# Forget gates by token-stationary matmuls, and two steps of the second attention layer in another place

## The chip, the core and the metric

The kernel runs on one core of a Trainium2 chip. The metric is the time on the device of one execution, in microseconds; of several runs the median counts. Five engines with an instruction queue each work side by side: TensorE (PE, with its weight loads shown apart as PEld), VectorE (DVE), ScalarE (ACT), GpSimd (POOL) and SyncE (SP, whose queue here issues nearly all DMAs). They wait for each other by semaphores.

## What is computed

Two blocks of a transformer for 256 tokens of width 1024, all in fp32: first a block with latent attention, a Fourier mixer and 32 experts, then two layers more, one that mixes two sparse attentions and has an MLP, and one with forgetting attention ("FoX") and an MLP. The change lies in the FoX layer. In the terms of the code, with h the normalised tokens (256 x 1024):

```
q, k, v, z = split(h @ odd_w_in)      # widths 1024, 1024, 1024, 16 (one z per head)
f   = log_sigmoid(z + b_forget)       # 256 x 16, as min(z, 0) - log(1 + exp(-|z|))
cum = cumsum(f, over tokens)
s[h, i, j] = q_i . k_j / 8 + cum[i, h] - cum[j, h]    for j <= i
out = softmax(s) @ v;   x = x + out @ odd_w_out
```

## The kernel before

The program is written engine by engine: each block (`block.tensor`, `block.vector` and so on) is the queue of one engine in the order in which it is written, and a step starts when those ahead of it in its queue are done and its `wait_ge` is met. There is no scheduler. Three stages follow each other; the last, `stage_second`, holds the two later layers.

Tokens lie on the free side: `hT` is [128 partitions, 8 chunks of the width, 256 tokens]. The helper `columns` (L1869) projects 128 output columns with 8 matmuls whose stationary side are weights and whose moving side is hT (256 columns); `tokens` (L1875) does it the other way, hT stationary and 512 weight columns moving. An fp32 matmul of the program stands as two in the profile.

The FoX layer begins when the MLP of the layer before has added its last pair of chunks to x. `fox("fq0")`, `fox("fk0")` and so on project the queries and keys of head pair 0, 1, ... into banks 2 and 3 of PSUM in turn; VectorE takes each out (`fox_query` L2594, `fox_key` L2597) and scales it. Between fq0 and fk0 stand the sums for the variance (`both_variances`, L1897 and L1905).

The gates go this way. L2162 computes z for both token blocks at once: per chunk of the width a matmul with 32 stationary columns (16 gate columns and the 16 before them in the weights) and hT moving, the chunks spread over four strips of 32 output partitions, so that each strip holds the sum over two of the eight. VectorE copies that to SBUF (`gate_part`, L2613). L2168 adds the four strips and turns z to tokens on partitions, by a matmul with the constant `gate16`. VectorE adds the bias (L2618) and forms |z| (L2620), ScalarE takes exp and log (L2354, L2356, each with a table load), VectorE ends with the log forget value `lf` (L2625). L2175 and L2178 form the cumulative sums, as matmuls with a triangle, in both layouts; VectorE takes them out (L2629, L2630).

`attn.scores` (L1500, with L1505 adding the cumulative sum of the keys) is followed on VectorE by `fox_biased` (L2605, then the maximum in L1512 and L1514), on ScalarE by exp (L1521) and on VectorE by the norm (L1527, L1535). `attn.turn` (L1546) transposes the probabilities on TensorE once the norm is done, ScalarE copies them to SBUF (L1554), and `weigh_f` (L1562, L1565) multiplies by the values.

On TensorE the order around the change is: fq0, variances, gate projection, fk0, sum of strips, fq1, fk1, cumulative sums, fq2, scores 0, fk2, scores 1, turn 12, v00 (the first half of the values). SyncE loads the gate weights (L1816) while the MLP before begins.

Of the kernel before, what the change touches and what calls it, by code (L numbers as in the profile page):

```python
# [15 lines left out]
P = 128  # L16
D = 1024
C = D // P
SEQ = 256
QT = SEQ // P  # L20
# [9 lines left out]
EXPERTS, TOPK, FF = 32, 4, 1024  # L30
# [26 lines left out]

CONST = {}
_at = 0
for _name, _n in (("ident", P), ("ones", P), ("tri", QT * SEQ), ("iota", P), ("causal", QT * SEQ), ("cmpvalid", QT), ("etri", EXPERTS), ("gate16", 16),  # L60
                  ("twin", HD), ("heads16", 8), ("swap", P), ("ccos", P), ("csin", P), ("stri", QT * SEQ),
                  ("cos", SEQ), ("sin", SEQ), ("ncos", QT * SEQ), ("nsin", QT * SEQ), ("quad", EXPERTS)):
    CONST[_name] = (_at, _n)
    _at += _n
# [4 lines left out]
def shape_constants():  # L69

    out = np.zeros((P, NCONST), np.float32)
    buckets = np.zeros((BUCKETS, 2, 512), np.float32)

    def put(name, a):
        a = np.asarray(a, np.float32)
        a = a.reshape(a.shape[0], -1)
        at, n = CONST[name]
        out[:a.shape[0], at:at + n] = a

    eye = np.eye(P)  # L80
    put("ident", eye)
    put("ones", np.ones((P, P)))
    swap = np.zeros((P, P))
    for i in range(P // 2):
        swap[2 * i + 1, 2 * i] = -1.0
        swap[2 * i, 2 * i + 1] = 1.0
    put("swap", swap)
    k = np.arange(HD)
    ang = 2 * np.pi * np.outer(k, k) / HD
    put("ccos", np.kron(np.eye(2), np.cos(ang)))  # L90
    put("csin", np.kron(np.eye(2), np.sin(ang)))
    n = np.arange(SEQ)
    incl = (n[:, None] <= n[None, :]).astype(np.float32).reshape(QT, P, SEQ).transpose(1, 0, 2)
    strict = (n[:, None] < n[None, :]).astype(np.float32).reshape(QT, P, SEQ).transpose(1, 0, 2)
    put("tri", incl)
    put("stri", strict)
    half = ROPE // 2
    inv = (1.0 / (np.float32(10000.0) ** (np.arange(0, half, 2, dtype=np.float32) / np.float32(half)))).astype(np.float32)
    row = (n // 64).astype(np.float32)
    col = (n % 64).astype(np.float32)  # L100
    a = np.concatenate([row[:, None] * inv, col[:, None] * inv], axis=-1)
    put("cos", np.tile(np.repeat(np.cos(a).T, 2, axis=0), (2, 1)))
    put("sin", np.tile(np.repeat(np.sin(a).T, 2, axis=0), (2, 1)))
    big = 2 * np.pi * (np.outer(n, n) % SEQ) / SEQ
    norm = 1.0 / math.sqrt(SEQ * HD)
    put("ncos", (np.cos(big) * norm).reshape(QT, P, SEQ).transpose(1, 0, 2))
    put("nsin", (-np.sin(big) * norm).reshape(QT, P, SEQ).transpose(1, 0, 2))
    put("iota", np.tile(np.arange(P), (P, 1)))
    nf = np.maximum(n, 1).astype(np.float32)
    large = 16 + (np.log(nf / np.float32(16)) / np.float32(math.log(64)) * np.float32(16)).astype(np.int32)  # L110
    bucket = np.where(n < 16, n, np.minimum(large, BUCKETS - 1))
    fwd = np.zeros((BUCKETS, 512))
    fwd[bucket, n + 256] = 1.0
    buckets[:, 0] = fwd[:, ::-1]
    buckets[:, 1] = np.where(np.arange(512) <= 255, 0.0, NEG)
    q = n[:, None]
    put("causal", np.where(n[None, :] <= q, 0.0, NEG).reshape(QT, P, SEQ).transpose(1, 0, 2))
    end = np.arange(NCMP) * CMP_STRIDE + CMP_BLOCK - 1
    seen = end[None, :] <= q
    put("cmpvalid", seen.any(1).astype(np.float32).reshape(QT, P).T)  # L120
    put("twin", (np.arange(P)[:, None] % HD == np.arange(HD)[None, :]).astype(np.float32))
    put("heads16", (np.arange(P)[:, None] // 16 == np.arange(8)[None, :]).astype(np.float32))
    e = np.arange(EXPERTS)
    put("gate16", (np.arange(P)[:, None] % EXPERTS - 16 == np.arange(16)[None, :]).astype(np.float32))
    put("quad", (np.arange(P)[:, None] % EXPERTS == e[None, :]).astype(np.float32))
    put("etri", (e[:, None] < e[None, :]).astype(np.float32))
    return out, buckets
# [46 lines left out]
def cst(m, name, rows=P, lo=0, n=None):  # L174
    at, width = CONST[name]
    src = m.consts
    if at >= LASTING:
        src, at = m.early, at - LASTING
    return src[0:rows, at + lo:at + (width if n is None else lo + n)]
# [1446 lines left out]
def stage_second(nc, m, t):  # L1626
# [4 lines left out]
    xT, hT, ps, ring = m.xT, m.hT, m.ps, m.ring  # L1631
# [47 lines left out]
    fv = valw[:, 0:2 * D].rearrange("p (i n) -> p i n", i=QT)  # L1679
    kcT, vcT, kslT, kwnT = (pairs[:, 2 * j:2 * j + 2, :] for j in range(4))  # L1680
    final_row = pairs[:, 0:4, :].rearrange("p a n -> p (a n)")
    wf = pairs[:, 4, :].rearrange("p (c h) -> p c h", c=C)
    bf = pairs[:, 5, 64:80]
    gate_part = std[:]
    z, e = (pairs[:, 5, 32 * j:32 * j + 32].rearrange("p (i h) -> p i h", i=QT) for j in range(2))
    lf = pairs[:, 6, :].rearrange("p (j n) -> p j n", j=QT)
    ncumT = pairs[:, 7, :]
# [32 lines left out]
    def place(name):  # L1720
# [15 lines left out]
    gates_ok, blocks_ok, vbd_ok = m.sem("ev_gates_ok"), m.sem("ev_blocks_ok"), m.sem("ev_vbd_ok")  # L1736
    c_ps, c_bias, c_peak, c_sub, c_exp, c_sum, c_inv, c_gated, c_ready, c_pt, c_taken = (
        m.sem(f"c_{n}") for n in ("ps", "bias", "peak", "sub", "exp", "sum", "inv", "gated", "ready", "pt", "taken"))
    st_ps, st_std, st_ok, fp_ps, fp_ok, fz_ps, z_ok, e_ok, lf_ok, cum_ps, cum_ok = (
        m.sem(f"od_{n}") for n in ("st_ps", "st_std", "st_ok", "fp_ps", "fp_ok", "fz_ps", "z_ok", "e_ok", "lf_ok", "cum_ps", "cum_ok"))  # L1740
    sems = [m.sem(f"turn_{n}") for n in ("pair_ps", "x_ok", "h_ok", "sq_ok", "acc_ok", "scaled")]
    pair_ps = sems[0]
    turns = [Turnover(m, n, sems, gain, banks, sq, acc[:]) for n, (gain, banks) in enumerate((
# [11 lines left out]
    with nc.Block() as block:  # L1755
# [10 lines left out]
        def _(sp):  # L1766
# [46 lines left out]
            sp.wait_ge(pair_ps, 4)  # L1813
            sp.dma_start(w_fq[0], odd[:, :, 0:512]).then_inc(fqk_in[0][0], 16)
            sp.dma_start(w_fk[0], odd[:, :, D:D + 512]).then_inc(fqk_in[1][0], 16)
            sp.dma_start(wf, odd[:, :, 3 * D - 16:]).then_inc(fox_in, 16)  # L1816
            sp.dma_start(bf, bcast_row(t["odd_b_forget_2"], 16)).then_inc(fox_in, 16)
            sp.dma_start(final_row, bcast_row(t["final_norm_2"], D)).then_inc(row_in, 16)
            mlp(0)
# [26 lines left out]
        def _(pe):  # L1846
# [291 lines left out]
            def fox(name, w, at, h_ready=known):  # L2138
                columns(fox_bank(name), w, at, h_ready, proj_ps)

            def scores_f(u):
                _, _, v = place(f"fq{u}")
                _, _, w = place(f"fk{u}")
                pe.wait_ge(got_v, max(v, w))
                if u == 0:
                    pe.wait_ge(cum_ok, 2)
                attn.scores(pe, 12 + u, fqT[:, u, :], fkT[:, u, :], lambda hd: (
                    cst(m, "ident", P, HD * hd + u, 1)[HD * hd:HD * (hd + 1), :].to_broadcast([HD, P]), ncumT[HD * hd:HD * (hd + 1), :]))
# [8 lines left out]
            both_variances(turns[2])  # L2157
            pe.wait_ge(fox_in, 32)
            pe.wait_ge(turns[2].x_ok, 12)
            for c in range(C):  # L2160
                q = 32 * (c % 4)
                mm = pe.matmul(ps[q:q + 32, 1, 0:SEQ], wf[:, c, :], hT[:, c, :], start=(c < 4), stop=(c >= 4))  # L2162
            mm.then_inc(fp_ps, 1)
            pe.wait_ge(fqk_in[1][0], 16)
            fox("fk0", w_fk[0], 0)
            pe.wait_ge(fp_ok, 1)
            for i in range(QT):
                mm = pe.matmul(ps[:, 0, i * 16:(i + 1) * 16], gate_part[:, i * P:(i + 1) * P], cst(m, "gate16"), start=True, stop=True)  # L2168
            mm.then_inc(fz_ps, 1)
            fox("fq1", w_fq[0], 128)  # L2170
            fox("fk1", w_fk[0], 128)
            pe.wait_ge(lf_ok, 2)
            for i in range(QT):
                for j in range(QT):
# [2 lines left out]
            for j in range(QT):  # L2177
                mm = pe.matmul(ps[:, 1, 0:SEQ], lf[:, j, :], cst(m, "tri", P, j * SEQ, SEQ), start=(j == 0), stop=(j == QT - 1))  # L2178
            mm.then_inc(cum_ps, 1)
            fox("fq2", w_fq[0], 256)  # L2180
            scores_f(0)
            fox("fk2", w_fk[0], 256)
            scores_f(1)
            attn.turn(pe, 12)
# [217 lines left out]
        def _(v):  # L2402
# [193 lines left out]
            def fox_key(u):  # L2596
                v.tensor_tensor(fkT[:, u, :], ps[:, fox_bank(f"fk{u}"), 0:SEQ], rb[:], ALU.mult).then_inc(got_v, 1)  # L2597
# [10 lines left out]
                attn.peak(v, n)  # L2608

            fox_query(0)  # L2610
            v.wait_ge(fp_ps, 1)
            v.wait_ge(st_ok, 5)
            v.tensor_copy(gate_part, ps[:, 1, 0:SEQ]).then_inc(fp_ok, 1)  # L2613
            fox_key(0)
            v.wait_ge(fz_ps, 1)
            v.wait_ge(fox_in, 32)
            for i in range(QT):
                v.scalar_tensor_tensor(z[:, i, :], ps[:, 0, i * 16:(i + 1) * 16], small[:, 4 + i:5 + i], bf, ALU.mult, ALU.add).then_inc(z_ok, 1)  # L2618
            v.wait_ge(z_ok, 2)
            v.scalar_tensor_tensor(e, z, -1.0, z, ALU.mult, ALU.max).then_inc(z_ok, 1)  # L2620
            fox_query(1)
            v.wait_ge(e_ok, 2)
            v.wait_ge(zeroed, 3)
            for i in range(QT):
                v.scalar_tensor_tensor(lf[:, i, :].rearrange("p (b q) -> p b q", b=2)[:, :, 0:8], z[:, i, :].rearrange("p (q b) -> p b q", b=2), 0.0,  # L2625
                                       e[:, i, :].rearrange("p (q b) -> p b q", b=2), ALU.min, ALU.subtract).then_inc(lf_ok, 1)
            fox_key(1)
            v.wait_ge(cum_ps, 1)
            v.tensor_copy(std[:], ps[:, 0, 32:32 + SEQ]).then_inc(cum_ok, 1)  # L2629
            v.tensor_scalar(ncumT, ps[:, 1, 0:SEQ], -1.0, None, ALU.mult).then_inc(cum_ok, 1)  # L2630
            v.wait_ge(cum_ok, 2)
            fox_query(2)
            fox_biased(0)
            attn.norm(v, 12)
            fox_key(2)
            fox_biased(1)
# [92 lines left out]
```

## Time and profile before

| | us |
|---|---|
| median of 3 runs | 1918.4 |
| lowest and highest | 1914.99, 1919.13 |
| profiled execution, its own time | 1918.4 |
| its span in the profile | 1916.6 |
| TensorE busy | 1845.6 |
| VectorE busy | 392.9 |
| ScalarE busy | 343.8 |

Busy is the time in which an engine has an instruction in work. A matmul's end in the profile is modelled and reaches into the next, so durations of matmuls can't be added; starts can be compared. "Idle before" stands behind an instruction in square brackets, with what ended it. "Chain" is the chain of work that ended last. PEclk is the clock granted to TensorE as a share of full speed: 1.00 is 2.4 GHz, 0.50 is 1.2 GHz.

### The profile page before, as it was taken

How to read it: one execution, taken by the hardware profiler on the slowest of the kernel's cores; microseconds unless marked ns; L12 is line 12 of the kernel's file. 1: busy time of each engine (PE TensorE's matmuls, PEld its weight loads, DVE VectorE, ACT ScalarE, POOL GpSimd, SP SyncE). 2: the span in 40 equal slices, each digit the busy share in tenths (PEclk: the TensorE clock that was granted, in tenths of full speed). 3: DMA queues.
4: the chain of work that ended last, by engine and by line, in shares of the span. 5: the costliest groups of instructions: out<-in, count | busy, mean ns of one | idle time of the engine just before them, and what ended most of it. 6: DMA issues, size and time to landing. Idle time of an engine off the chain costs nothing. (4 is left out here: it accounts for less than half of the span.)

```text
span 1916.6 us, 22073 instructions
## 1 busy us (share of the span) xinstructions
PE 1845.6 (96%) x8901; PEld 1051.5 (55%) x8902; DVE 392.9 (21%) x819; ACT 343.8 (18%) x675; POOL 5.3 (0%) x10
## 2 busy tenths in 40 slices
PE   6999799999999999999999997999999999999998
PEld 4857433333333333333333336678888876776664
DVE  1754411111111101111111115542000043110001
ACT  2222311111111111111111113322000032120001
POOL 0000000000000000000000000000000000000000
PEclk9999799999999999999999998999999999999999
DMA  9986499999999999999999996435244413314331
GB/s 400 313 200 278 167 406 431 430 431 432 432 432 432 430 431 432 432 432 432 430 431 431 432 418 182 165 132 190 90 173 175 175 44 132 132 44 176 138 125 66
DMA packets 100587, 558.31 MB, mean 291 GB/s; under 512 B 16600, under 2 KB 33469, under 8 KB 73789
## 3 DMA queue, kind: packets, MB, share of 16 engines
q1 hardware_dynamic: 98084, 553.17, 70.5%
q10 hardware_dynamic: 2458, 4.50, 1.8%
q8 instruction: 33, 0.54, 0.1%
q14 instruction: 12, 0.10, 0.0%
HBM read 552.41 MB, written 5.23 MB: 291 GB/s over the span
## 5 line engine op out<-in xcount | busy, mean ns | idle before, releaser
L1338 PE MATMUL ps<-ring,xs 128*64 128x512 f32 x2112 | 466.7, 593 | 7.7 <-DMA ring<-in_w_up 4.7
L1338 PEld LDWEIGHTS ps<-ring,xs 128*64 128x64 f32 x2112 | 150.8, 137 | 311.8 <-issue 293.6
L1391 PE MATMUL ps<-ring,actT 128*64 128x512 f32 x1056 | 233.9, 595 | 0.0
L2074 PE MATMUL ps<-hT,ring 128*128 128x256 f32 x1024 | 223.9, 379 | 0.2 <-ACT hT L1588 0.2
L2074 PEld LDWEIGHTS ps<-hT,ring 128*128 128x128 f32 x1024 | 194.3, 190 | 29.6 <-issue 2.9
L1391 PEld LDWEIGHTS ps<-ring,actT 128*64 128x64 f32 x1056 | 72.9, 137 | 158.7 <-issue 131.9
L1869 PE MATMUL ps<-hT,ring 128*128 128x256 f32 x512 | 118.6, 386 | 6.1 <-ACT hT L1588 4.9
L1463 DVE TENSOR_SCALAR hT<-ps 128x512 f32<-128x512 f32 x33 | 22.8, 692 | 446.8 <-PE ps L1338 446.8
L2084 PE MATMUL ps<-ring 128*128 128x256 f32 x512 | 111.6, 379 | 0.0
L2097 PE MATMUL ps<-ring 128*128 128x512 f32 x256 | 111.0, 592 | 0.0
L1869 PEld LDWEIGHTS ps<-hT,ring 128*128 128x128 f32 x512 | 96.4, 192 | 23.6 <-issue 9.5
L2084 PEld LDWEIGHTS ps<-ring 128*128 128x128 f32 x512 | 97.3, 190 | 13.2
L2568 DVE TENSOR_TENSOR ring<-ring 128x1024 f32<-128x1024 f32 x16 | 19.6, 1226 | 356.8 <-ACT ring L2338 356.8
L2338 ACT ACTIVATE ring<-ps 128x1024 f32<-128x1024 f32 x16 | 16.4, 1024 | 363.1 <-PE ps L2074 363.1
L2097 PEld LDWEIGHTS ps<-ring 128*128 128x128 f32 x256 | 48.6, 190 | 58.2 <-issue 57.9
L1465 DVE TENSOR_SCALAR hT<-ps 128x512 f32<-128x512 f32 x33 | 22.8, 692 | 266.2 <-PE ps L1338 266.2
L1348 PE MATMUL ps<-selT,y 64*128 64x256 f32 x544 | 67.9, 389 | 0.7 <-ACT y L1437 0.7
L1306 PE MATMUL ps<-x_sb,sel 128*64 128x512 f32 x272 | 65.9, 606 | 1.7 <-DVE sel L1446 1.7
L1437 ACT COPY y<-ps 128x512 f32<-128x512 f32 x33 | 19.3, 586 | 246.5 <-PE ps L1391 246.5
L1430 ACT COPY xs<-ps 128x512 f32<-128x512 f32 x33 | 19.4, 586 | 235.1 <-PE ps L1312 235.1
L2045 PE MATMUL ps<-x_sb,ring 128*128 128x256 f32 x256 | 57.4, 381 | 0.9 <-ACT x_sb L1571 0.9
L1348 PEld LDWEIGHTS ps<-selT,y 64*128 64x128 f32 x544 | 49.7, 186 | 11.6 <-issue 5.5
(411 smaller groups left out, 1456.6 us busy)
## 6 DMA issues: line engine op xcount, KB each, us to landing
ring<-in_w_up SPq DMA_DIRECT2D x64, 2048.0 KB, 23.0
ring<-in_w_down SPq DMA_DIRECT2D x64, 2048.0 KB, 24.1
ring<-in_w_gate SPq DMA_DIRECT2D x64, 2048.0 KB, 22.5
ring<-in_mlp_w SPq DMA_DIRECT2D x32, 2048.0 KB, 7.8
ring<-in_w_mod SPq DMA_DIRECT2D x8, 2048.0 KB, 17.1
ring<-in_odd_w_in SPq DMA_DIRECT2D x6, 2048.0 KB, 7.6
ring<-in_w_mod SPq DMA_DIRECT2D x8, 1024.0 KB, 14.3
ring<-in_even_w_in SPq DMA_DIRECT2D x4, 2048.0 KB, 15.9
```

The costliest lines, as they stand in the source:

```text
L1306: mm = pe.matmul(ps[SLOTS * half:SLOTS * (half + 1), TURN, :], sel[:, i, :], h2[:, i, half * 512:(half + 1) * 512], start=(i == 0), stop=( ...
L1338: mm = pe.matmul(ps[SLOTS * half:SLOTS * (half + 1), bank, :], xs[:, c % 4, c // 4 * SLOTS:(c // 4 + 1) * SLOTS], weights(v, 8 * part + c) ...
L1348: mm = pe.matmul(ps[:, COMB + 2 * half + j // 2, (j % 2) * SEQ:(j % 2 + 1) * SEQ], y[SLOTS * half:SLOTS * (half + 1), j * P:(j + 1) * P], ...
L1391: mm = pe.matmul(ps[SLOTS * half:SLOTS * (half + 1), Y, :], actT[:, f % 4, f // 4 * SLOTS:(f // 4 + 1) * SLOTS], weights(v, 16 + f)[:, hal ...
L1463: v.tensor_scalar(g, ps[:, G, :], LIMIT, None, ALU.min).then_inc(g_ok, 1)
L1465: v.tensor_scalar(u, ps[:, U, :], -LIMIT, LIMIT, ALU.max, ALU.min).then_inc(u_ok, 1)
L1869: mm = pe.matmul(ps[:, bank, 0:SEQ], w[:, c, at:at + P], hT[:, c, :], start=(c == 0), stop=(c == C - 1))
L2045: mm = pe.matmul(ps[:, turn.banks[k], (d % 2) * SEQ:(d % 2 + 1) * SEQ], w_out[:, c, d * P:(d + 1) * P], mixT[:, c, :], start=(first and c ...
L2074: mm = pe.matmul(ps[:, UP[layer][b] + f // 2, (f % 2) * SEQ:(f % 2 + 1) * SEQ], mlp_w1[b][:, c, f * P:(f + 1) * P], hT[:, c, :], start=(c ...
L2084: mm = pe.matmul(ps[:, turns[2].banks[k], (d % 2) * SEQ:(d % 2 + 1) * SEQ], mlp_w2[b][:, f, d * P:(d + 1) * P], sqr4[:, b, f, :], start=(f ...
L2097: mm = pe.matmul(ps[:, 2 + 2 * i + half, :], sqr4[:, b, f, i * P:(i + 1) * P], mlp_w2[b][:, f, half * 512:(half + 1) * 512], start=(first ...
L2568: v.tensor_tensor(sqr4[:, b], relu4[:, b], relu4[:, b], ALU.mult).then_inc(sqr_ok, 1)
```

## The change

The gate projection now is made with hT stationary: for each of the two blocks of 128 tokens, eight matmuls with a 128x128 stationary piece of hT and the 16 gate columns moving, which add up in PSUM to z with tokens on partitions. The matmuls that added strips, the copy between, the constant `gate16` and two semaphores are gone. The loaded weights have 16 columns per chunk where they had 32.

In the order of TensorE's queue the cumulative sums stand ahead of fk1 where they stood behind it, and scores 0 ahead of fq2. VectorE's queue follows: |z| then fk0, lf then fq1, the sums' copies then fk1, the bias of scores 0 then fq2.

```
-    ("etri", EXPERTS), ("gate16", 16),
+    ("etri", EXPERTS),
...
-    wf = pairs[:, 4, :].rearrange("p (c h) -> p c h", c=C)
-    bf = pairs[:, 5, 64:80]
-    gate_part = std[:]
+    wf = pairs[:, 4, 0:C * 16].rearrange("p (c h) -> p c h", c=C)
+    bf = pairs[:, 4, 128:144]
...
-            sp.dma_start(wf, odd[:, :, 3 * D - 16:]).then_inc(fox_in, 16)
+            sp.dma_start(wf, odd[:, :, 3 * D:]).then_inc(fox_in, 16)
...
-            for c in range(C):
-                q = 32 * (c % 4)
-                mm = pe.matmul(ps[q:q + 32, 1, 0:SEQ], wf[:, c, :], hT[:, c, :], start=(c < 4), stop=(c >= 4))
-            mm.then_inc(fp_ps, 1)
+            for i in range(QT):
+                for c in range(C):
+                    mm = pe.matmul(ps[:, 0, i * 16:(i + 1) * 16], hT[:, c, i * P:(i + 1) * P], wf[:, c, :], start=(c == 0), stop=(c == C - 1))
+            mm.then_inc(fz_ps, 1)
             pe.wait_ge(fqk_in[1][0], 16)
             fox("fk0", w_fk[0], 0)
-            pe.wait_ge(fp_ok, 1)
-            for i in range(QT):
-                mm = pe.matmul(ps[:, 0, i * 16:(i + 1) * 16], gate_part[:, i * P:(i + 1) * P], cst(m, "gate16"), start=True, stop=True)
-            mm.then_inc(fz_ps, 1)
             fox("fq1", w_fq[0], 128)
-            fox("fk1", w_fk[0], 128)
             pe.wait_ge(lf_ok, 2)
...
             mm.then_inc(cum_ps, 1)
+            fox("fk1", w_fk[0], 128)
+            scores_f(0)
             fox("fq2", w_fq[0], 256)
-            scores_f(0)
             fox("fk2", w_fk[0], 256)
...
             fox_query(0)
-            v.wait_ge(fp_ps, 1)
-            v.wait_ge(st_ok, 5)
-            v.tensor_copy(gate_part, ps[:, 1, 0:SEQ]).then_inc(fp_ok, 1)
-            fox_key(0)
```

TensorE's queue from fq0 to the first transposes, before (128x256 x8 is a projection of 128 columns; numbers are those of the program, half of the profile's):

```order
L1869 MATMUL ps<-hT,ring 128x256 x8
L1905 MATMUL ps<-consts_sb,acc 128x1 x4
L2162 MATMUL ps<-hT,ring 32x256 x8
L1869 MATMUL ps<-hT,ring 128x256 x8
L2168 MATMUL ps<-consts_sb,std 128x16 x2
L1869 MATMUL ps<-hT,ring 128x256 x16
L2175 MATMUL ps<-ring,consts_sb 128x128 x4
L2178 MATMUL ps<-consts_sb,ring 128x256 x2
L1869 MATMUL ps<-hT,ring 128x256 x8
L1500 MATMUL ps<-ring 128x128 x2
L1505 MATMUL ps<-ring,consts_sb 128x256 x2
L1869 MATMUL ps<-hT,ring 128x256 x8
```

The same place after (lines stand two to seven lower):

```order
L1867 MATMUL ps<-hT,ring 128x256 x8
L1903 MATMUL ps<-consts_sb,acc 128x1 x4
L2160 MATMUL ps<-ring,hT 128x16 x16
L1867 MATMUL ps<-hT,ring 128x256 x16
L2168 MATMUL ps<-ring,consts_sb 128x128 x4
L2171 MATMUL ps<-consts_sb,ring 128x256 x2
L1867 MATMUL ps<-hT,ring 128x256 x8
L1499 MATMUL ps<-ring 128x128 x2
L1504 MATMUL ps<-ring,consts_sb 128x256 x2
L1867 MATMUL ps<-hT,ring 128x256 x16
```

The 8 matmuls with 32 stationary columns and the 2 behind fk0 are replaced by 16 with 16 moving columns; fk0 and fq1 now follow each other, one projection stands between the cumulative sums and scores 0, and fq2 and fk2 stand together behind these.

VectorE's queue from fq0's evacuation to the norm of pair 0, before:

```order
L2594 SCALAR_TENSOR_TENSOR ring<-ps,rb 128x256
L2613 COPY std<-ps 128x256
L2597 TENSOR_TENSOR ring<-ps,rb 128x256
L2618 SCALAR_TENSOR_TENSOR ring<-ps,small,ring 128x16
L2620 SCALAR_TENSOR_TENSOR ring<-ring 128x32
L2594 SCALAR_TENSOR_TENSOR ring<-ps,rb 128x256
L2625 SCALAR_TENSOR_TENSOR ring<-ring 128x2x8
L2597 TENSOR_TENSOR ring<-ps,rb 128x256
L2629 COPY std<-ps 128x256
L2594 SCALAR_TENSOR_TENSOR ring<-ps,rb 128x256
L2605 SCALAR_TENSOR_TENSOR ring<-ps,std,consts_sb 128x128
L1527 RECIPROCAL top<-top 128x4
```

And after:

```order
L2588 SCALAR_TENSOR_TENSOR ring<-ps,rb 128x256
L2608 SCALAR_TENSOR_TENSOR ring<-ps,small,ring 128x16
L2610 SCALAR_TENSOR_TENSOR ring<-ring 128x32
L2591 TENSOR_TENSOR ring<-ps,rb 128x256
L2615 SCALAR_TENSOR_TENSOR ring<-ring 128x2x8
L2588 SCALAR_TENSOR_TENSOR ring<-ps,rb 128x256
L2619 COPY std<-ps 128x256
L2591 TENSOR_TENSOR ring<-ps,rb 128x256
L2599 SCALAR_TENSOR_TENSOR ring<-ps,std,consts_sb 128x128
L2588 SCALAR_TENSOR_TENSOR ring<-ps,rb 128x256
L1526 RECIPROCAL top<-top 128x4
```

The copy of the strips is gone, each projection is taken out one step later against the gate's chain, and fq2 is taken out between the bias and the norm of pair 0.

## Rows read from the trace of the kernel before

**Rows 1.** Page, busy us of each engine: the row of TensorE

```profile
PE 1845.6 (96%) x8901; PEld 1051.5 (55%) x8902; DVE 392.9 (21%) x819; ACT 343.8 (18%) x675; POOL 5.3 (0%) x10
```

**Rows 2.** Stretches: from:to, length, busy us of each engine, clock, DMA

```profile
1541.00:1571.00 30.00, 29.41 (x173) 23.96 (x172) 11.98 (x32) 10.25 (x20) 0.00 (x0) 1.00 0.18 68
1690.00:1915.00 225.00, 219.18 (x775) 144.84 (x773) 15.73 (x17) 14.41 (x19) 0.00 (x0) 1.00 0.31 116
```

**Rows 3.** Timeline, TensorE's matmuls: start us, us, engine, line, operation, tiles, shapes

```profile
1544.10 0.95 PE L1905 MATMUL ps<-consts_sb,acc 128*128 128x1 f32 x8
1544.98 1.07 PE L2162 MATMUL ps<-hT,ring 128*32 128x256 f32 x16
1545.98 3.72 PE L1869 MATMUL ps<-hT,ring 128*128 128x256 f32 x16
1549.54 0.51 PE L2168 MATMUL ps<-consts_sb,std 128*128 128x16 f32 x4
1549.90 7.15 PE L1869 MATMUL ps<-hT,ring 128*128 128x256 f32 x32
1556.89 1.05 PE L2175 MATMUL ps<-ring,consts_sb 128*128 128x128 f32 x8
1558.65 3.62 PE L1869 MATMUL ps<-hT,ring 128*128 128x256 f32 x16
1562.19 0.49 PE L1500 MATMUL ps<-ring 64*128 64x128 f32 x4
1563.71 3.72 PE L1869 MATMUL ps<-hT,ring 128*128 128x256 f32 x16
```

**Rows 4.** Line 657 (ns min/median/max, first and last start), and line 2007 in the chain

```profile
L657 PEld LDWEIGHTS ps<-wr,modc x16: 190/190/192, 186.5 to 188.3; 128*128 128x128 f32 x16
L657 PE MATMUL ps<-wr,modc x16: 193/276/276, 186.7 to 188.3; 128*128 128x32 f32 x16
...
1246.00 1.89 PE ps L2007 x32
```

**Rows 5.** Timeline, weight loads that open scores 1, v00, scores 2, v01

```profile
1567.36 0.30 PEld L1500 LDWEIGHTS ps<-ring 64*128 64x128 f32 x4 [0.33 <-issue]
...
1570.08 0.30 PEld L1875 LDWEIGHTS ps<-ring,hT 128*128 128x128 f32 x2
...
1577.14 0.30 PEld L1500 LDWEIGHTS ps<-ring 64*128 64x128 f32 x4 [0.76 <-issue]
...
1579.26 0.30 PEld L1875 LDWEIGHTS ps<-ring,hT 128*128 128x128 f32 x2
```

**Rows 6.** Timeline, VectorE and ScalarE: fk0's evacuation, gates, sums, bias, norm

```profile
1549.74 0.42 DVE L2597 TENSOR_TENSOR ring<-ps,rb 128x256 f32<-128x256 f32 x1 [2.36 <-PE ps L1869]
...
1552.27 0.32 ACT L2356 ACTIVATE ring<-ring,one 128x32 f32<-128x32 f32 x1
...
1553.64 0.42 DVE L2594 SCALAR_TENSOR_TENSOR ring<-ps,rb 128x256 f32<-128x256 f32 x1 [2.94 <-PE ps L1869]
1553.98 0.25 DVE L2625 SCALAR_TENSOR_TENSOR ring<-ring 128x16 f32<-128x16 f32 x2
...
1559.19 0.41 DVE L2630 TENSOR_SCALAR ring<-ps 128x256 f32<-128x256 f32 x1
...
1568.61 1.03 DVE L1535 TENSOR_TENSOR ring<-ring,top 128x256 f32<-128x256 f32 x2
```

**Rows 7.** The gate weights' load: issue (first and last start), time to landing

```profile
L1816 SPq DMA_DIRECT2D ring<-in_odd_w_in x1: 3377/3377/3377, 1318.6 to 1318.6; - x1
...
DMA to landing us min/median/max: 12.1/12.1/12.1
```

**Rows 8.** Timeline behind an idle TensorE, and stretches after it (columns of rows 2)

```profile
1172.64 0.59 PE L1500 MATMUL ps<-ring 64*128 64x128 f32 x2 [2.48 <-DVE ring L2433]
...
1177.00:1178.00 1.00, 1.00 (x3) 0.72 (x3) 0.00 (x0) 1.00 (x7) 0.00 (x0) 0.50 1.09 387
...
1179.00:1181.00 2.00, 2.00 (x10) 1.58 (x9) 0.00 (x0) 0.25 (x1) 0.00 (x0) 0.98 0.59 209
```

More of the change, by code:

```diff
@@ L59 @@
 _at = 0
-for _name, _n in (("ident", P), ("ones", P), ("tri", QT * SEQ), ("iota", P), ("causal", QT * SEQ), ("cmpvalid", QT), ("etri", EXPERTS), ("gate16", 16),
+for _name, _n in (("ident", P), ("ones", P), ("tri", QT * SEQ), ("iota", P), ("causal", QT * SEQ), ("cmpvalid", QT), ("etri", EXPERTS),
                   ("twin", HD), ("heads16", 8), ("swap", P), ("ccos", P), ("csin", P), ("stri", QT * SEQ),
@@ L123, in shape_constants @@
     e = np.arange(EXPERTS)
-    put("gate16", (np.arange(P)[:, None] % EXPERTS - 16 == np.arange(16)[None, :]).astype(np.float32))
     put("quad", (np.arange(P)[:, None] % EXPERTS == e[None, :]).astype(np.float32))
@@ L1738, in stage_second @@
         m.sem(f"c_{n}") for n in ("ps", "bias", "peak", "sub", "exp", "sum", "inv", "gated", "ready", "pt", "taken"))
-    st_ps, st_std, st_ok, fp_ps, fp_ok, fz_ps, z_ok, e_ok, lf_ok, cum_ps, cum_ok = (
-        m.sem(f"od_{n}") for n in ("st_ps", "st_std", "st_ok", "fp_ps", "fp_ok", "fz_ps", "z_ok", "e_ok", "lf_ok", "cum_ps", "cum_ok"))
+    st_ps, st_std, st_ok, fz_ps, z_ok, e_ok, lf_ok, cum_ps, cum_ok = (
+        m.sem(f"od_{n}") for n in ("st_ps", "st_std", "st_ok", "fz_ps", "z_ok", "e_ok", "lf_ok", "cum_ps", "cum_ok"))
     sems = [m.sem(f"turn_{n}") for n in ("pair_ps", "x_ok", "h_ok", "sq_ok", "acc_ok", "scaled")]
@@ L2620, in _ @@
             v.scalar_tensor_tensor(e, z, -1.0, z, ALU.mult, ALU.max).then_inc(z_ok, 1)
-            fox_query(1)
+            fox_key(0)
             v.wait_ge(e_ok, 2)
@@ L2626, in _ @@
                                        e[:, i, :].rearrange("p (q b) -> p b q", b=2), ALU.min, ALU.subtract).then_inc(lf_ok, 1)
-            fox_key(1)
+            fox_query(1)
             v.wait_ge(cum_ps, 1)
@@ L2630, in _ @@
             v.tensor_scalar(ncumT, ps[:, 1, 0:SEQ], -1.0, None, ALU.mult).then_inc(cum_ok, 1)
+            fox_key(1)
             v.wait_ge(cum_ok, 2)
+            fox_biased(0)
             fox_query(2)
-            fox_biased(0)
             attn.norm(v, 12)
```

## The prediction

> **What bounds the kernel now.** I read the page's engine table first: TensorE is busy 1845.6 of 1916.6 us [rows 1]. Two questions follow: is it also the engine that sets the end where the change works, and what would a slower step there be hidden behind? The table of stretches answers the first: in the 30 us in which the second attention layer starts, TensorE works 29.41 us at a granted clock of 1.00, while VectorE works 11.98 and ScalarE 10.25; in the last 225 us, from the second MLP on, it works 219.18 [rows 2]. The timeline of TensorE answers the second: from 1544.10 to 1567.36 one group of matmuls starts where the one before leaves off, with no wait for another engine in it [rows 3]. So here a microsecond of TensorE is a microsecond of the kernel, and work of the other engines counts only where it makes TensorE wait. What comes behind is a chain of matmuls too, so nothing absorbs a delay.
>
> The change does two things. It computes the forget gates in another way on TensorE, and it moves two other steps (the cumulative sums ahead of fk1, the scores of head pair 0 ahead of fq2). I price each on TensorE's own timeline, from the start of a group's first matmul to that of the next group. Each matmul of the program stands twice in the profile.
>
> **The gate projection before.** Eight 32-column matmuls of hT (L2162, 16 in the profile) run from 1544.98 to 1545.98: 1.00 us. The two that add up the four partial results (L2168) run from 1549.54 to 1549.90: 0.36 us [rows 3]. Together 1.36 us go.
>
> **The gate projection after.** There are 2 x 8 = 16 matmuls, 32 in the profile, each with a 128x128 weight load of hT and only 16 moving columns. Such a form isn't in this stretch in number, so I bound it. The nearest rows are L657, 128x128 weights with 32 moving columns: 16 of them with starts from 186.7 to 188.3, so 1.6/15 = 0.107 us each [rows 4]. L1905, one moving column, takes 1544.10 to 1544.98 for 8, 0.110 each, and L2168, 16 columns, 0.36/4 = 0.09 [rows 3]. All say that the weight load sets the pace, not the columns. From below: L2007 runs 32 in 1.89 us, 0.059 each [rows 4], but with weights of 64 rows in alternating halves, so it may overlap loads as the new ones cannot. From above: a load lasts 190 ns [rows 4]; if none overlapped, 32 x 0.190 = 6.08 us. I take L657's 0.107, the nearest form: 32 x 0.107 = 3.42 us. Ends: 1.89 and 6.08.
>
> At this point a page of the Trainium skill speaks against the change. "TensorEngine Tiling (Array Packing)", Performance Considerations, advises for a right operand of at most 64 columns to swap it to the stationary side and to use column tiles; that is what the kernel before does and the change undoes. The rows on either form agree with it as to sign: 1.36 against 3.42 us. The same page (Tiling Modes, Key Properties) says that a change of tiling mode drains the engine. The change removes two such switches, and if each gave back the 0.17 us by which L657's modelled 276 ns outlasts its pace, the sum would be 0.3 us lower. The trace gives no reason for it: 1.00 us holds the switches already, and fk0 behind them takes 3.56 us where fq2 takes 3.54.
>
> **The walk from 1544.98 to the scores of pair 1.** Before, these start at 1567.36, 22.38 us later [rows 5]. After, with pieces of the same trace [rows 3]:
> gate 3.42, so fk0 starts at 1548.40;
> fk0 and fq1 in one piece behind short matmuls, as fq1 and fk1 did (1549.90 to 1556.89): 6.99, to 1555.39;
> cumulative sums 1556.89 to 1558.65: 1.76, to 1557.15;
> fk1 behind them, as fq2 did (1558.65 to 1562.19): 3.54, to 1560.69;
> scores 0 (1562.19 to 1563.71): 1.52, to 1562.21;
> fq2 behind scores, as fk2 did (1563.71 to 1567.36): 3.65, and fk2 with no break, half of 6.99 less the 0.1 of a start: 3.4, to 1569.3.
> That is 24.3 against 22.4: 1.9 us later.
>
> **What the move gives back.** Before, the transposes of pair 0 (turn 12) come too early: from the weight load that opens scores 1 (1567.36) to that which opens v00 (1570.08) pass 2.72 us. The same three steps for the next pair take 1577.14 to 1579.26 = 2.12 us [rows 5]. The difference, 0.60, is the wait for the normalised probabilities, whose last is written at 1568.61 + 1.03 = 1569.64 [rows 6]. That is 1569.64 - 1562.19 = 7.45 after scores 0 began. After the change scores 0 start at 1560.69, the probabilities are there at 1568.14, and the transposes are due at 1569.3 + 1.52 = 1570.8. VectorE now takes fq2 between the bias and the norm, but fq2 ends 3.7 us behind its start at 1562.21, so it is evacuated by 1566.4, while exp ends at the latest when the norm begins, by 1568.61, 6.4 us after scores 0 began, so by 1567.1. The wait goes whole: 0.60 us. Next late would be nothing: the norm of pair 1 follows with 7 us of v00 as cover.
>
> **The waits that remain.** The cumulative sums wait for the log forget values (lf_ok). Before they are written at 1553.98 + 0.25 = 1554.23 and asked for at 1556.89. After: the logarithm ended at 1552.59, 2.54 after the last gate matmul's modelled end of 1550.05; so now at about 1548.6 + 2.5 = 1551.1. VectorE stands in its queue at fk0's evacuation, which comes 1549.74 - 1545.98 = 3.76 after fk0's start, so at 1552.16, and lf follows 0.34 behind (1553.64 to 1553.98), written by 1552.75 [rows 6]. TensorE asks at 1555.39: 2.6 us in hand. Scores 0 wait for the sums' copies: 1559.60 - 1556.89 = 2.71 after their start, so at 1558.10, asked for at 1560.69: again 2.6 in hand. Queued behind them on TensorE is all the rest, so if either margin were gone each missing microsecond would cost one; both are far from it. The removed copy on VectorE (L2613) cost nothing, since VectorE waited for fk0 afterwards, and gives nothing.
>
> **Loads and layout at nothing.** The gate weights' load halves its row to 64 bytes with as many rows. It is issued at 1318.6 and landed 12.1 us later [rows 7]; it is wanted at 1545. More than 200 us of MLP hide it, and would hide it at twice the time. The constants are 16 columns shorter, which moves later buffers by 64 bytes. No row shows a price for an address; the three runs of before, 1914.99 to 1919.13, bound what I could see of it: 0, with 2 us either way.
>
> **Sum.** + 1.9 - 0.6 = + 1.3 us. The profiled execution took 1918.4 us (span 1916.6 and 1.8 around it), which is also the median of the runs, so 1919.7. With the gate's ends of 1.89 and 6.08 us it is 1918.2 and 1922.4.
>
> **Rivals.**
> First, the clock (slower). Behind the variance matmuls with one column the new gate stands with 16: 40 short matmuls in a row, 0.88 + 3.42 = 4.3 us in which TensorE does little but load weights. The trace has a fall of the granted clock to 0.50, the 1.2 GHz level: scores at 1172.64 follow a wait of 2.48 us, the clock is 0.50 at 1177 and back at 0.98 from 1179 [rows 8]. If the gate's stretch worked on the clock as an idle one, some 7 us (1172 to 1179) would run at half speed and lose 3.5 us: 1.3 + 3.5 = 4.8, 1923.2 us. It decides if the granted clock in 1545 to 1555 leaves 1.00. Against it: the engine is never idle there, and short matmuls (L657's 1.7 us, L2007's 1.9) lie where the clock stays at 1.00, but none of these lasts 4 us.
> The Trainium skill, "TensorE: Matmul & The Clock Gate", Part 1, says that the gate follows how busy the array was of late; whether weight loads count as busy it doesn't say. By the reading that they don't, this rival holds.
> Second, loads that overlap as L2007's do: gate 1.89 us, sum -0.2, 1918.2 us. For it: only that row. Against: L657 and L1905 have this form and don't.
> Third, the wait at turn 12 stays although scores 0 come earlier, as when VectorE's queue (fq2 ahead of the norm) holds it: + 1.9, 1920.3 us. Against it are the 2.6 us in hand.
> Fourth, the new order pays more than I see, or the shifted buffers do, so that the kernel is faster: it would need 5 us on TensorE against the walk. No wait of that size stands in this stretch: the largest is the 0.60.
>
> **How the numbers follow.** A measurement of this kernel tells from no change about 0.2%, 3.8 us. Forecast 0.73, clock 0.11, overlapping loads 0.06, wait that stays 0.06, more gain 0.04. The forecast and both middle rivals lie within 3.8 us; of their 0.85 I give 0.01 to slower for a gate near its upper end and 0.02 to faster, since the runs of before spread by 4 us; the clock rival is slower by 4.8 us but may be smaller, of its 0.11 I leave 0.01 to no change. Faster 0.06, same 0.83, slower 0.11. The range goes from 1915.5 (the lower rival less the runs' spread) to 1923 (gate at its upper end, and most of the clock rival).
>
> **What would show it.** In the profile after: the gate's 32 matmuls in 3.2 to 3.6 us at clock 1.00; no wait ahead of the cumulative sums; scores 0 at about 1560.7 on the old scale; turn 12 directly behind scores 1, with 2.1 us from the opening of scores 1 to that of v00; v00 1.3 us later than before, and the last MLP equally so. Wrong would make me a clock of 0.50 in that stretch, a gate of 2 or of 6 us, or a change of the span whose place lies outside 1545 to 1571.

## The result: slower by half a percent, in two places

The changed kernel takes 1928.68 us (median of 6 runs, 1926.95 to 1929.18) against 1918.43 of the kernel before (6 runs, 1914.99 to 1919.87). The ratio is 1.0054, 95% interval 1.0043 to 1.0064. That is ten microseconds more, where I forecast 1.3, and it lies outside my range. The profiled execution has a span of 1925.7 us, 9.1 more than before.

Two landmarks split the 9.1 us. The first is the variance sums just ahead of the gate. The timeline of TensorE in the changed kernel (start us, us, engine, line, operation) answers to [rows 3]:

```profile
1548.46 0.95 PE L1903 MATMUL ps<-consts_sb,acc 128*128 128x1 f32 x8
1549.27 4.64 PE L2160 MATMUL ps<-ring,hT 128*128 128x16 f32 x32
1553.74 9.59 PE L1867 MATMUL ps<-hT,ring 128*128 128x256 f32 x32
1563.17 1.05 PE L2168 MATMUL ps<-ring,consts_sb 128*128 128x128 f32 x8
1564.93 3.62 PE L1867 MATMUL ps<-hT,ring 128*128 128x256 f32 x16
1568.47 0.49 PE L1499 MATMUL ps<-ring 64*128 64x128 f32 x4
1569.98 7.17 PE L1867 MATMUL ps<-hT,ring 128*128 128x256 f32 x32
```

The variance sums started at 1544.10 before and start at 1548.46 now: 4.36 us are lost before anything that I had priced. The second landmark is the weight load that opens v00, at 1570.08 before [rows 5]. TensorE's weight loads after, where scores 1, turn 12 and v00 open:

```profile
1577.09 0.30 PEld L1499 LDWEIGHTS ps<-ring 64*128 64x128 f32 x4 [0.33 <-issue]
...
1578.60 0.64 PEld L1545 LDWEIGHTS ps<-consts_sb,ring 128*128 128x128 f32 x6 [0.33 <-issue]
1579.20 0.30 PEld L1873 LDWEIGHTS ps<-ring,hT 128*128 128x128 f32 x2
```

It is 9.12 later, the whole difference of the spans; so 4.8 us are lost between the landmarks and nothing behind them.

**Between the landmarks: the clock.** The gate takes 1553.74 - 1549.27 = 4.47 us where I had 3.42, and fk0 with fq1 take 9.43 where the same two took 6.99. All behind them is as in the walk: 1.76 for the sums, 3.54 for fk1, 1.51 for scores 0, 7.11 for fq2 with fk2. The stretches of the changed kernel (from:to, length, busy of PE, PEld, DVE, ACT, POOL, granted clock, DMA share, GB/s):

```profile
1549.00:1551.00 2.00, 2.00 (x20) 2.00 (x19) 1.80 (x3) 1.67 (x3) 0.00 (x0) 1.00 0.93 345
1551.00:1552.00 1.00, 1.00 (x10) 1.00 (x10) 0.40 (x1) 0.01 (x1) 0.00 (x0) 0.93 0.01 2
1552.00:1557.00 5.00, 5.00 (x17) 4.37 (x18) 0.57 (x3) 2.38 (x4) 0.00 (x0) 0.50 0.01 3
1557.00:1559.00 2.00, 2.00 (x7) 1.61 (x6) 0.00 (x0) 0.74 (x1) 0.00 (x0) 0.58 0.00 0
1559.00:1563.00 4.00, 4.00 (x21) 3.51 (x20) 0.59 (x3) 0.00 (x0) 0.00 (x0) 1.00 0.00 0
```

The clock falls to its lower level, 1.2 GHz, shortly before 1552, in the middle of the gate, while TensorE is busy without a break, and is back before 1559. In [rows 2] it was 1.00 throughout. The length of a stretch times what its clock lacks of 1.00 is what the low clock takes from it: 0.07 x 1 + 0.50 x 5 + 0.42 x 2 = 3.4 us. The weight loads show the same:

```profile
1549.24 1.87 PEld L2160 LDWEIGHTS ps<-ring,hT 128*128 128x128 f32 x16
...
1551.81 1.99 PEld L2160 LDWEIGHTS ps<-ring,hT 128*128 128x128 f32 x9
```

Less the last load's 0.19 us, that is 1.68/15 = 0.112 us from load to load at full clock and 1.80/8 = 0.225 at half. The price at full clock was right; the clock was not.

**Ahead of the landmarks: the expert stage.** In the experts' stage the matmuls run on weights that have just come in, and the DMA engines have no rest: their busy share, the last figure but one of a stretch, is 1.01. The same stretch, before and then after:

```profile
330.00:1100.00 770.00, 759.77 (x3846) 288.10 (x3844) 106.00 (x252) 128.45 (x194) 0.00 (x0) 1.00 1.01 431
```

```profile
330.00:1100.00 770.00, 756.05 (x3824) 286.20 (x3822) 105.54 (x251) 128.41 (x194) 0.00 (x0) 1.00 1.01 428
```

The loads come at 428 GB/s where they came at 431. The weight loads and matmuls of the up and gate projections before (first and last start; then what the weight loads waited for, us in all, times):

```profile
L1338 PE MATMUL ps<-ring,xs x2112: 592/592/643, 235.9 to 1134.8; 128*64 128x512 f32 x192
...
  DMA ring<-in_w_up: 16.1, 16
  DMA ring<-in_w_gate: 9.0, 10
```

And after:

```profile
L1337 PE MATMUL ps<-ring,xs x2112: 592/592/643, 236.7 to 1140.3; 128*64 128x512 f32 x192
...
  DMA ring<-in_w_up: 23.2, 22
  DMA ring<-in_w_gate: 15.7, 20
```

The stage is 903.6 us long in place of 898.9, 4.7 more, with more waits for weights; its code is the same. It begins 0.8 us later and so ends 5.5 us later, of which 1.1 are given back before the landmark. There the clock is at its lower level for a few microseconds in either trace, but not in the same place: from 1174 to 1178 it is 0.50 before and 1.00 after. So the 4.36 us hold for these two executions; the runs below say better what the stage costs.

### The profile page after: what moved, and what is told of

Read it like the earlier page. It is cut to its first block and busy times, and to the rows that moved or that the text cites. A ratio compares the mean times of both kernels' runs of the same rounds, so it can differ in the third digit from the quotient of the medians.

```text
span 1925.7 us, 22094 instructions
## 1 busy us (share of the span) xinstructions
PE 1851.7 (96%) x8913; PEld 1056.5 (55%) x8914; DVE 392.8 (20%) x818; ACT 343.9 (18%) x675; POOL 5.3 (0%) x10
## 5 line engine op out<-in xcount | busy, mean ns | idle before, releaser
L1337 PE MATMUL ps<-ring,xs 128*64 128x512 f32 x2112 | 467.5, 593 | 11.6 <-DMA ring<-in_w_up 6.9
L1337 PEld LDWEIGHTS ps<-ring,xs 128*64 128x64 f32 x2112 | 150.5, 137 | 316.9 <-issue 288.9
```

Of the source, the lines that this page charges most:

```text
L1337: mm = pe.matmul(ps[SLOTS * half:SLOTS * (half + 1), bank, :], xs[:, c % 4, c // 4 * SLOTS:(c // 4 + 1) * SLOTS], weights(v, 8 * part + c) ...
```

## The experiments

Ratios are to the kernel before, with 95% intervals. "Old layout" means that 16 unused columns stand where `gate16` stood, so that all buffers lie as before.

**1. The change in the old layout.** For this and the next kernel the edit is one of the constants alone:

```
-... ("etri", EXPERTS),
+... ("etri", EXPERTS), ("gap", 16),
```

> The changed kernel, with 16 unused columns kept in the constants where gate16 stood, so that every later buffer and the width of the constants are as before. Theory (two causes: the clock's fall at the gate costs about 4.8 us, and the shifted buffers slow the loads of the experts' weights by about 5 us): the expert stage goes back to before, 1923 us, ratio 1.0025. Rival (the expert stage's 5 us are a variation between executions, or come with the code itself): 1928 us, ratio 1.005. Both: granted clock 0.50 for about 7 us at the gate.

Measured: 1923.89 us, ratio 1.0029 (1.0018 to 1.0039). The expert stage is back:

```profile
330.00:1100.00 770.00, 759.41 (x3844) 287.87 (x3842) 105.51 (x251) 128.44 (x194) 0.00 (x0) 1.00 1.01 431
```

The clock falls as in the changed kernel, to 0.50 from 1548 to 1554. So the layout is one cause, and the other lies in the gate or the order.

**2. The layout without the change.**

```
-("gate16", 16),
...
-cst(m, "gate16")
+cst(m, "quad", P, 16, 16)
```

> The kernel before, with gate16 read from columns 16 to 31 of the constant quad (same numbers) and its own 16 columns gone, so that the constants and all later buffers lie as in the changed kernel; nothing else differs. Theory (shift slows the expert loads): 1923 us, ratio 1.0025, the DMA rate in the expert stage 428 GB/s instead of 431, clock 1.00 at the gate. Rival (variation between executions, or the code): 1918 us, ratio 1.000.

Measured: 1922.7 us, ratio 1.0023 (1.0013 to 1.0033), 429 GB/s, clock 1.00 at the gate. Sixteen columns of constants less, and nothing else, cost about four microseconds. Together with run 1 that is 0.23 + 0.29 = 0.52%, the 0.54 of the whole.

**3. The order alone.**

```
+            fox("fk1", w_fk[0], 128)
+            scores_f(0)
             fox("fq2", w_fq[0], 256)
-            scores_f(0)
```

(with fk1 taken from ahead of the sums, the strips' matmuls left where they were, and VectorE's queue as in the change)

> The kernel before with only the two steps moved (cumulative sums ahead of fk1, scores 0 ahead of fq2, VectorE's queue to match), the old gate projection and the old layout. Theory (the move takes away the wait ahead of turn 12 and costs nothing): 0.6 us less, 1917.8, ratio 0.9997; from the opening of scores 1 to that of v00 2.12 us in place of 2.72. Rival (the old gate's longer chain through the strips' copy makes the sums wait for lf): up to 2 us more, and a wait ahead of the sums.

Measured: 1917.71 us, ratio 0.9992 (0.9983 to 1.0002). The times can't tell it from the kernel before, but the trace shows the step. Weight loads of this kernel:

```profile
1568.79 0.30 PEld L1500 LDWEIGHTS ps<-ring 64*128 64x128 f32 x4 [0.33 <-issue]
...
1570.91 0.30 PEld L1875 LDWEIGHTS ps<-ring,hT 128*128 128x128 f32 x2
```

From scores 1 to v00 pass 2.12 us, against 2.72 in [rows 5]: the 0.60 is gained. The sums wait for nothing, and the rival falls. The clock is 1.00 from 1540 to 1575.

**4. The gate alone**, in the old order and the old layout.

```
-                mm = pe.matmul(ps[q:q + 32, 1, 0:SEQ], wf[:, c, :], hT[:, c, :], ...)
+                    mm = pe.matmul(ps[:, 0, i * 16:(i + 1) * 16], hT[:, c, i * P:(i + 1) * P], wf[:, c, :], ...)
```

> The kernel before with only the new gate projection (hT stationary, 16 moving columns), the old order and the old layout (16 unused columns kept). Theory (short matmuls bring the clock down): +1.9 us for the matmuls (32 at 0.107 for 1.36), +0.1 to 0.2 for the tail at half speed, +3.4 for what follows at half speed: 1923.5, ratio 1.0028, clock 0.50 for about 7 us. Rival (the clock falls because of the new order and not of the gate): clock 1.00, 1920.5, ratio 1.001.

Measured: 1924.21 us, ratio 1.0031 (1.002 to 1.0042). Stretches from the gate on:

```profile
1546.00:1549.00 3.00, 3.00 (x30) 3.00 (x28) 2.20 (x3) 2.02 (x3) 0.00 (x0) 1.00 0.83 324
1549.00:1551.00 2.00, 2.00 (x14) 2.00 (x13) 0.00 (x0) 0.00 (x0) 0.00 (x0) 0.65 0.03 8
1551.00:1557.00 6.00, 6.00 (x17) 4.84 (x17) 0.57 (x3) 3.12 (x4) 0.00 (x0) 0.55 0.00 0
```

The clock falls with the gate alone, and takes the same 3.4 us (0.35 x 2 + 0.45 x 6); with the order alone (run 3) it doesn't fall. The order has no part in it.

**5 and 6. Where the layout acts.** Run 5 shifts the buffers in the core's memory and keeps the array of constants in main memory; run 6 shortens that array and puts a pad ahead of the ring.

```
run 5:  +    return np.concatenate([out, np.zeros((P, 16), np.float32)], axis=1), buckets
run 6:  +    m.pad = m.sb("pad", [P, 16])
             m.ring = m.sb("ring", [P, 4 * PARTS, D])
```

> The kernel before with gate16 read from quad, so that in the core's memory the constants are 16 columns shorter and all later buffers lie 64 bytes lower, while the array of constants in the chip's main memory keeps its old width (16 unused columns at the end of each row, not loaded). Theory (the place of the ring in the core's memory slows the expert loads): as the shifted kernel before, 1922.7, ratio 1.0023, expert stage 428 to 429 GB/s. Rival (what lies where in main memory does it): ratio 1.000, 431 GB/s.

> The counterpart: the constants are 16 columns shorter in main memory and in the core, but a pad of 16 columns ahead of the ring puts it and all later buffers where they were. Theory (place of the ring): ratio 1.000, 431 GB/s. Rival (place in main memory): ratio 1.0023, 428 to 429 GB/s.

Measured: run 5 1923.19 us, ratio 1.0022 (1.0013 to 1.0031), 428 GB/s; run 6 1919.11 us, 0.9999 (0.999 to 1.0008), 431 GB/s. So it is the place of the buffers in the core's memory. The ring and all buffers behind it move together in these runs; it is the ring that the experts' weights are loaded into. The stretch of run 5, then of run 6:

```profile
330.00:1100.00 770.00, 756.48 (x3826) 286.69 (x3824) 105.53 (x251) 128.16 (x194) 0.00 (x0) 1.00 1.01 428
```

```profile
330.00:1100.00 770.00, 759.26 (x3844) 287.83 (x3842) 105.47 (x251) 128.34 (x194) 0.00 (x0) 1.00 1.01 431
```

**7. As many weight loads, more columns.**

```
-mm = pe.matmul(ps[:, 0, i * 16:(i + 1) * 16], hT[...], wf[:, c, :], ...)
+mm = pe.matmul(ps[:, 0, i * P:(i + 1) * P].rearrange("p (a n) -> p a n", a=8), hT[...],
+               wf[:, c, :].rearrange("p (a n) -> p a n", a=1).to_broadcast([P, 8, 16]), ...)
```

> The changed kernel in the old layout, where each gate matmul moves its 16 columns eight times over (128 moving columns, 7 of 8 results not read): as many weight loads as in the changed kernel, and as each load takes 0.107 us and 128 columns do too (the cumulative sums run 8 such in 0.89), the same 3.4 to 3.6 us at full clock. Theory (the clock falls since the array gets few columns): clock stays 1.00, +1.5 us to before, 1921, ratio 1.0008. Rival (the clock falls because of the 32 weight loads, or this much stationary data from hT): 0.50 for 7 us as before, ratio 1.0026 and more.

Measured: 1920.34 us, ratio 1.0004 (0.9995 to 1.0013). Timeline of TensorE, and the stretches:

```profile
1546.57 0.95 PE L1903 MATMUL ps<-consts_sb,acc 128*128 128x1 f32 x8
1547.38 3.82 PE L2160 MATMUL ps<-ring,hT 128*128 128x128 f32 x32
1551.04 7.07 PE L1867 MATMUL ps<-hT,ring 128*128 128x256 f32 x32
1557.94 1.05 PE L2169 MATMUL ps<-ring,consts_sb 128*128 128x128 f32 x8
```

```profile
1549.00:1551.00 2.00, 2.00 (x20) 2.00 (x19) 0.48 (x3) 0.12 (x1) 0.00 (x0) 1.00 0.05 15
1551.00:1553.00 2.00, 2.00 (x12) 1.77 (x12) 0.57 (x3) 1.11 (x2) 0.00 (x0) 1.00 0.00 0
```

Eight times the columns through the array, of which seven eighths are thrown away, and the kernel is faster than run 1: the interval ends at 1.0013 where that of run 1 begins at 1.0018. The gate takes 3.66 us and fk0 with fq1 6.90, at clock 1.00. The loads, their number and their data are those of run 1. The moving columns, and with them the results written, are all that differs: 16 where the clock fell, 128 where it didn't. What is left is the walk of the prediction with 3.66 in place of 3.42. The weight load that opens v00 stands 27.41 us behind the variance sums:

```profile
1573.98 0.30 PEld L1873 LDWEIGHTS ps<-ring,hT 128*128 128x128 f32 x2
```

**8. Two short stretches in place of one.**

```
+            gate_half(0)
             pe.wait_ge(fqk_in[1][0], 16)
             fox("fk0", w_fk[0], 0)
+            gate_half(1).then_inc(fz_ps, 1)
```

> The changed kernel in the old layout, with the gate of the first 128 tokens ahead of fk0 and that of the other 128 behind it, two stretches of 1.7 us in place of one of 3.4. Theory (the length of the stretch of short matmuls decides, together with the 0.9 us of variance matmuls ahead): clock 1.00 in both, +1.4 us, ratio 1.0007. Rival (their total in some longer time decides): the clock falls all the same, ratio 1.0025.

Measured: 1922.32 us, ratio 1.0013 (1.0004 to 1.0022), between both expectations. In the execution traced the clock falls all the same, behind the variance's matmuls (0.81 us) and the first half (1.79 us), but for half as long: it takes 1.7 us (0.28 x 2 + 0.50 x 2 + 0.05 x 3). fk0 takes 5.22 us (1547.02 to 1552.24) for 3.55, and the second half runs at full clock.

```profile
1545.00:1547.00 2.00, 2.00 (x20) 2.00 (x20) 1.83 (x3) 1.65 (x3) 0.00 (x0) 1.00 0.89 346
1547.00:1549.00 2.00, 2.00 (x9) 1.64 (x9) 0.37 (x1) 0.00 (x0) 0.00 (x0) 0.72 0.03 8
1549.00:1551.00 2.00, 2.00 (x6) 1.58 (x5) 0.00 (x0) 0.00 (x0) 0.00 (x0) 0.50 0.00 0
1551.00:1554.00 3.00, 3.00 (x23) 2.82 (x21) 0.00 (x0) 0.00 (x0) 0.00 (x0) 0.95 0.00 0
```

**9 and 10. Which places are slow.** A pad of 64, and of 32, columns ahead of the ring of the kernel before.

> The kernel before with a pad of 64 columns ahead of the ring: the ring then starts at byte 32768 of a partition. By the program's own addresses it started at 32512 before (a multiple of 256, not of 512), and at 32448 in the changed kernel (a multiple of 64 only). Theory (the start against multiples of 256 is what the loads feel): same as before, ratio 1.000, 431 GB/s. Rival (multiples of 512 are better still, or any move is worse): 0.998 or less, or 1.002.

> The kernel before with a pad of 32 columns: the ring starts at 32640, a multiple of 128 and not of 256. Theory (256): slow as the shift of 64 bytes, ratio 1.002, 428 to 429 GB/s. Rival (only starts off a multiple of 128 are slow): ratio 1.000, 431 GB/s.

Measured: 1920.1 us, ratio 1.0001 (0.9992 to 1.001), 431 GB/s, and 1923.2 us, 1.0024 (1.0015 to 1.0033), 428 GB/s. So of four places, 32512 and 32768 (multiples of 256) are fast and 32448 and 32640 are slow by the same amount. The traces of all runs fall into the same two groups: from first to last matmul of L1338 (L1337 in some kernels) the four slow ones (the changed kernel, runs 2, 5 and 10) take 902.5 to 903.6 us and the ten others 898.8 to 900.2. The stretch of run 10:

```profile
330.00:1100.00 770.00, 756.37 (x3826) 286.48 (x3824) 105.51 (x251) 128.41 (x194) 0.00 (x0) 1.00 1.01 428
```

The Trainium skill has a rule that fits. "DMA: Bandwidth & Descriptors", How a descriptor splits into AXI transactions, says that a descriptor is cut into transactions of 256 bytes, and that for one which doesn't start at a multiple of 256 bytes the first transaction starts at the multiple below, and the bytes in between are fetched for nothing and still cost steps of the transfer (beats). It says so of reads. Here it is the written side that moved, and runs 2, 5 and 10 lose 2 to 3 in 431; that the reason is the same was not shown.

**11. The gate spread over fk0.**

```
+            def gate_step(c):
+                i, k0 = c // 4, 2 * (c % 4)
+                for k in (k0, k0 + 1):
+                    mm = pe.matmul(ps[:, 0, i * 16:(i + 1) * 16], hT[:, k, i * P:(i + 1) * P], wf[:, k, :], ...)
-            fox("fk0", w_fk[0], 0)
+            fox("fk0", w_fk[0], 0, gate_step)
```

> The changed kernel in the old layout, with the gate's 16 matmuls spread over fk0, two ahead of each of its eight chunks: the same instructions, no stretch of short ones but the variance's 0.9 us. Theory (the clock falls since a long stretch gives the array few columns): clock 1.00, +1.3 to 1.5 us, ratio 1.0007 as with 128 columns. Rival (two short matmuls in each 0.64 us keep columns too few over some time): the clock falls, +3 us or more, ratio 1.0015 and more.

Measured: 1920.71 us, ratio 1.0006 (0.9997 to 1.0015). The stretches, then the variance sums and the weight load that opens v00, again 27.41 us apart:

```profile
1546.00:1550.00 4.00, 4.00 (x33) 3.82 (x31) 2.20 (x3) 2.02 (x3) 0.00 (x0) 1.00 0.66 257
1550.00:1554.00 4.00, 4.00 (x28) 3.75 (x28) 0.32 (x2) 0.00 (x0) 0.00 (x0) 1.00 0.01 4
```

```profile
1546.08 0.95 PE L1903 MATMUL ps<-consts_sb,acc 128*128 128x1 f32 x8
...
1573.49 0.30 PEld L1873 LDWEIGHTS ps<-ring,hT 128*128 128x128 f32 x2
```

The very matmuls of the change, among long ones, leave the clock at 1.00. The mean granted clock of a whole execution bears this out beyond the executions traced: it is 0.985 to 0.987 in every one of the changed kernel and of runs 1 and 4, and 0.987 to 0.990 in every one of runs 3, 7 and 11.

**12. Old gate, new order, ring at a multiple of 512.**

> The best of both: old gate, new order, ring at byte 32768. Theory (the order is worth 0.6 us, the place nothing): ratio 0.9993 to 0.9997, about 1918.3. Rival (the place pays too): 0.998 or less.

Measured: 1919.18 us, ratio 0.9996 (0.9987 to 1.0005). From scores 1 to v00 again 2.11 us. It and run 3 are the best that the runs point to, and neither can be told from the kernel before. Against the changed kernel they are about 10 us faster, and that by leaving out what slows it.

## Why the prediction was wrong, step by step

**Step "loads and layout at nothing": this failed, and it is about 4 of the 10 us.** I wrote that no row shows a price for an address, and allowed 2 us either way from the spread of the runs. A shift off the multiples of 256 bytes costs 0.22 to 0.24% in three kernels (runs 2, 5, 10), 4.2 to 4.6 us by the ratios and 3.1 to 3.7 by the medians, and nothing that can be told where the ring stays on a multiple of 256 (runs 3, 6, 9). I had looked at the layout as something that touches instructions; it touches the 2 MB loads of the experts, whose stage has its DMA share at 1.01. The bound was wrong too: the spread of runs says how well a time is known, not how large an effect may be. The ends of the range don't come out either: 1918.2 less 2 us is 1916.2, less the whole spread of 4.1 it is 1914.1, and I wrote 1915.5; the upper end of 1923 lies below the clock rival's own 1923.2.

**Step "the walk at full clock": this failed too, and it is 3.3 us.** The walk priced the gate at 3.42 us and fk0 with fq1 at 6.99 with the clock at 1.00; they took 4.47 and 9.43. From the variance sums to the opening of v00 pass 30.74 us in the changed kernel and 30.76 in run 1, and 27.41 in runs 7 and 11, where the clock stays up: 3.3 us, beside the 3.4 that the stretches give.

**Rival "the clock": it held, and had 0.11.** Its price was 3.5 us, and its sum of 4.8 over the kernel before is the 4.8 that are lost between the landmarks. That price was borrowed from another fall (1172 to 1179), and nothing said beforehand that the new one would last as long; so the close match is in part luck. Runs 7 and 11 show what it hangs on: neither idle time nor weight loads, but short matmuls in a row. What I held against it, that the engine is never idle there and that 1.7 and 1.9 us of short matmuls leave the clock alone, was true and spoke only of shorter stretches. Run 8 had 0.8 us of variance sums with 1.8 of the gate, and fell in the execution traced. The length and the neighbours should have had more weight than the resemblance.
The Trainium skill's "TensorE: Matmul & The Clock Gate", Part 1, leaves open whether weight loads count as busy. Here they did not keep the clock up: PEld is busy throughout 1549 to 1552 in the changed kernel, and the clock falls.

**Gate at full clock.** Right: 0.112 us a load against 0.107, and 3.66 us for all in run 7 against 3.42. The ends of 1.89 and 6.08 weren't needed.

**The turn's wait.** Right: 2.11 to 2.12 us for 2.72, in the changed kernel and in runs 3 and 12. That the rival with a late VectorE would hold it back is refuted.

**The waits that remain.** Right: no wait stands ahead of the sums or of scores 0, in the changed kernel too, although half the clock made fk0 late; it made fq1 late as well, and with it the moment at which TensorE asks.

**The drain at a change of tiling mode.** Small if it is there. The Trainium skill's rule as I priced it took 0.3 us from the walk. In run 7 the variance sums ahead of the gate take 0.81 us for 0.88 and fk0 with fq1 behind it 6.90 for 6.99: 0.16 in all, about half of that, and no run tells whether it comes from the mode.

**The sum.** What I forecast is what is left when both misses are taken out. From the variance sums to the opening of v00 the kernel before takes 25.98 us and runs 7 and 11 take 27.41: 1.43 more, where I had 1.3. The two misses are the terms that I had put at nothing. In the traces they are 4.36 and 3.33 us, with 1.43 for the rest 9.12, which is the whole difference of the spans; the medians differ by 10.2.

## What to carry to other kernels

Before a constant or a small buffer is taken out, look at what is allocated behind it: if a large DMA destination starts on a multiple of 256 bytes, keep it there, and print the addresses of both versions. Short matmuls should stand among long ones, not in a row: the same 32 cost 3.3 us more in one block than spread over a projection, and here even useless columns were cheaper than few. Where one engine's stage is fed at the DMA's limit, ask of every edit, however far from it, whether it moves the buffers of that stage.

## What the hardware showed that I had not expected

The granted clock went to 0.50 with TensorE busy without a gap, some 2.6 us into 32 weight loads with 16 moving columns each, behind 8 with one, and stayed there for about 7 us of dense work. With 128 moving columns the same loads left it at 1.00.
The loads of 2 MB with rows of 16 KB ran at 431 GB/s into a ring that starts at 32512 or 32768 bytes and at 428 to 429 into one at 32448 or 32640; 64 bytes less per row in main memory did nothing that can be told (run 6, 0.9999).
